# Two token mixers in a fused float32 block: when the row scans run, in which order the mLSTM's heads go, and where the output projection's first terms stand

## The chip, the cores and the metric
The kernel runs on one core of one Trainium2 chip. The time is the device time of one execution in microseconds; the runs of the kernel before are 2084.67 (median), 2084.38 and 2088.93.

## The reference
All arithmetic is float32, on 256 tokens of width 1024. Two layers each do a feed-forward (SwiGLU, inner width 2816), a token mixer and a second feed-forward, each with modulation, residual and layer norm; then an attention block and a gated linear attention block follow. The change touches the two token mixers alone:

```python
qkv_a, a_a, b_a, z_a, qkv_b, qk_c, v_c, i_c, f_c, o_c = jnp.split(h @ w_in, IN_SPLITS, axis=-1)
qa, ka, va = jnp.split(causal_conv_silu(qkv_a, gdn_conv), 3, axis=-1)   # 6 heads of 64
qa, ka = l2norm(split_heads(qa)), l2norm(split_heads(ka))
oa = gated_delta_rule(qa, ka, va, g, beta)        # then rms over a head, norm gain, times silu(z_a)
ob = moba_attention(qb, kb, vb)                   # here: causal softmax attention, 4 heads
hc = mlstm_chunkwise(qc, kc, vc, i_pre, logf)     # 6 heads; num / max(|den|, exp(-m))
hc = hc * sigmoid(o_c)                            # then mean and variance over a head, gain
return jnp.concatenate([oa, ob, hc], axis=-1) @ w_out
```

## The kernel before, in words
Each engine has its own instruction stream, written out by hand, with semaphores between them; `step(...)` looks up the count at which a named step of another engine is done. All weights come as one stream of 1 MB chunks (2048 floats on each of 128 partitions) through a ring of 8 slots. The sync engine issues the loads in order, chunk n as soon as chunk n - 8 has been released. Every float32 product is issued as `mm`, two matmul instructions in the trace, all at L335; transposes are at L338. ScalarE's operations are all at L1253, VectorE's at L1720 (tensor with tensor), L1723 (with a scalar), L1726 (both) and L1729 (copy).

A mixer (`mixer(l)`, one function per engine, m = 1 and m = 4) works feature-major: a chunk of `w_in` gives two tiles of 128 features by 256 tokens.
- **Start.** The chunks of WIN_FIRST (12: gate rows; 0 to 4: the delta rule's q, k, v) are projected one after the other. VectorE convolves each tile (four operations, `conv`), ScalarE applies silu. `rows` (L2009) is VectorE's work on the gate rows: scans, maxima, a reciprocal. The l2 norm of q and k is square (ScalarE, "l2sq"), sums over a head (TensorE, "l2", six products), plus epsilon (VectorE, "l2e"), then reciprocal root as Ln and Exp (ScalarE, "ri", each with its own activation table). TensorE issues l2 behind the fourth chunk after 12 (i == 4), then the last chunk, then waits for "rows", the convolutions and "l2e" before it transposes the rows and spreads them over partitions ("pairs", "gb").
- **Middle.** The delta rule's 64 by 64 triangular inverses are built by five doubling steps (li = 1 to 5) of 48 small products and two half-updates each; the steps after it ("x" 6, "y" 6, "vn0", "s", "ks", "vn1", "oa", "oa_sum") are a chain between TensorE and VectorE or ScalarE.
- **Work beside the chain.** `BESIDE` is a list of pieces of independent work; each engine's `fill(n)` does the next n of them, and the places of the calls fix the order. Piece s writes its result to bank 0 (s even) or bank 7 (s odd) and waits until piece s - 2 has been read ("fread"). Kinds: p = half a chunk projected (p15 only 128 columns); ms, mt, mo = attention's scores, transposes, output; lm = exp of the mLSTM's minus maximum for a pair of heads; lb = one head's decay, two tiles of 256 and 128 columns; ls = its scores; ln and ld = numerator and denominator of a pair of heads. At the pieces numbered in `MOD_AT`, a column of the next sublayer's modulation is taken from a chunk on which GpSimd or VectorE worked, and that chunk's slot becomes free.
- **Tail.** For ld of pair p, VectorE takes max(-den, exp(-m)), max(den, that), a reciprocal (L1992), numerator times that, times the output gate ("lh"): five operations. After the third pair come "lmu" (head means), "lvar" (head variances) and the output projection: of its 8 terms in k, five (delta rule and attention) are issued first for all four chunks of `w_out`, the last three when "mixed" is there. Banks 0 to 3 hold its result.

Of the kernel before, what the change touches and what calls it, by code (L numbers as in the profile page):

```python
# [13 lines left out]
P = 128  # L14
# [24 lines left out]
WIN_FIRST = [12, 0, 1, 2, 3, 4]  # L39
WIN_LATER = [6, 7, 13, 8, 9, 10, 14, 15, 5, 11]  # L40
BESIDE = (["p6.0", "p6.1", "p7.0", "p7.1", "p13.0", "p13.1"]
# [4 lines left out]
HALVES = 4  # L46
FFN_ORDER = [c for p in range(FT // 2 + 1) for c in
             ((("w13", 2 * p), ("w13", 2 * p + 1)) if p < FT // 2 else ()) + ((("w2", p - 1),) if p else ())]
AFTER_MS = {"p8.0": 0, "p8.1": 1, "p9.0": 2, "p9.1": 3}
MOD_AT = {1: 2, 5: 3, 11: 4, 15: 5, 19: 6, 23: 7}  # L50
ROW_A, ROW_B, ROW_I, ROW_F = 0, 32, 64, 96
# [39 lines left out]
def build(nc, stream, cols_in, tab_in, wg_in, xt_in, ct_in, out, marks):  # L91
# [3 lines left out]
    with ExitStack() as ctx:  # L95
# [46 lines left out]
        def step(*key):  # L142

            return marks[key][1] if marks else 1
# [184 lines left out]
        def _(eng):  # L329
# [138 lines left out]
            def mixer(l):  # L468
# [25 lines left out]
                def part(name):  # L494
# [10 lines left out]
                    if kind == "p":  # L505
# [4 lines left out]
                        if t:  # L510
                            held[0] = held_w[1]
                            release()
                            found["beside", m, s] = found["chunk", held[0]]
                            return
                    elif kind == "ms":
                        h = int(what)
# [17 lines left out]
                    elif kind == "lm":  # L534
                        p = int(what)
                        mm(beside(s, 256), table("pair", P * p, P)[ROW_I:ROW_I + 32, :], r_nm[ROW_I:ROW_I + 32, :], True, True)
                    elif kind == "lb":
                        h = int(what)
                        mm(beside(s, 256), each(ident[ROW_I:ROW_I + 32, ROW_I + h:ROW_I + h + 1], 128)[:, 0, :], r_max[ROW_I:ROW_I + 32, :], True, True)
                    elif kind == "ls":  # L540
                        h = int(what)
                        o = beside(s)
                        eng.wait_ge(scalar_done, step("silu", m, 21))
                        mm(o[:, 0:256], head(qkv[:, 12:15], h, 0), head(qkv[:, 9:12], h), True, True)
                        mm(o[:, 256:384], head(qkv[:, 12:15], h, 1), head(qkv[:, 9:12], h, 1), True, True)
                    else:
                        for h in (2 * int(what), 2 * int(what) + 1):
                            o = half(beside(s, 256), h)
                            eng.wait_ge(vector_done, step("lp", m, h))
                            for st in range(2):  # L550
                                lhs = vt[:, st, 256 + 64 * h:256 + 64 * h + 64] if kind == "ln" else ones[:, 0:64]
                                if st == 0:
                                    mm(o, lhs, l_w[:, h, 0:256], True, False, free=True)
                                else:
                                    mm(o[:, P:T], lhs, l_w[:, h, 256:384], False, True, free=True)
                    last[0].then_inc(tensor_done, 1)
# [9 lines left out]
                for i, ch in enumerate(WIN_FIRST):  # L566
# [9 lines left out]
                    if i == 4:  # L576
# [6 lines left out]
                        done.named("l2", m)  # L583
                        mod_cols(m + 1, 1)

                eng.wait_ge(vector_done, step("rows", m))
# [131 lines left out]
                done.named("vn1", m)  # L718
                fill(2)
                eng.wait_ge(vector_done, step("vn1s", m))  # L720
# [8 lines left out]
                done.named("oa", m)  # L729
                fill(4)  # L730
                eng.wait_ge(scalar_done, step("oa_sq", m))
# [3 lines left out]
                done.named("oa_sum", m)  # L735
                fill(len(BESIDE) - at["n"])
                eng.wait_ge(vector_done, step("lh", m, 2))
# [3 lines left out]
                done.named("lmu", m)  # L741

                w_out, w_held = [], []
                eng.wait_ge(vector_done, step("oa_done", m))
                eng.wait_ge(scalar_done, step("mo", m, 1))
                for ch in range(4):
                    w_out.append(tiles(take("wout", l, ch), 256))
                    w_held.append(held[0])
                    for t in range(2):
                        for k in range(5):  # L750
                            mm(bank(ch, 256 * t, 256 * t + 256), w_out[ch][:, k, P * t:P * t + P], xa[:, k, CS], k == 0 and t == 0, False, free=True)
                    if ch == 0:
                        eng.wait_ge(scalar_done, step("lsq", m))
                        for t in range(3):
                            mm(banks(4, 1024)[:, 256 * t:256 * t + 256], blk, tiles(l_sq, 256)[:, t], True, True)
                        last[0].then_inc(tensor_done, 1)
                        done.named("lvar", m)
                eng.wait_ge(vector_done, step("mixed", m))
# [489 lines left out]
        def _(eng):  # L1248
# [107 lines left out]
            def mixer(l):  # L1356
# [18 lines left out]
                def part(s):  # L1375
# [5 lines left out]
                    if kind == "p":  # L1381
# [5 lines left out]
                        if ch < 13:  # L1387
                            gate_or_copy(2 * ch + t, beside(s, 256), *key)
                        else:
                            n = 256 if ch < 15 else 128  # L1390
                            act(vt[:, t, 256 * (ch - 13):256 * (ch - 13) + n], beside(s, n), ACT.Copy, *key).then_inc(scalar_done, 1)
                    elif kind == "ms":
                        h = int(what)
# [45 lines left out]
                act(g_sq, W(QKV, 1536), ACT.Square, "l2sq", m).then_inc(scalar_done, 1)  # L1439
                silu(6)  # L1440
                silu(7)
                eng.wait_ge(vector_done, step("l2e", m))
                rsqrt(g_tt, "ri", m)
                eng.wait_ge(tensor_done, step("proj", m, 5))
                gate_or_copy(9, bank(6, 256, 512), "proj_read_a", m, 5)
                silu(8)
                eng.wait_ge(tensor_done, step("pairs", m))
                eng.wait_ge(vector_done, step("kb", m))
# [23 lines left out]
                for b in range(2):  # L1472
                    act(tiles(g_tt, 128)[64 * b:64 * b + 64, :, 64 * b:64 * b + 64], tiles(g_tp, 64)[64 * b:64 * b + 64], ACT.Copy, "t", m, 7, b).then_inc(scalar_done, 1)
                fill(4)
                fill(8)
                eng.wait_ge(tensor_done, step("oa", m))
# [234 lines left out]
        def _(eng):  # L1711
# [211 lines left out]
            def mixer(l):  # L1923
# [28 lines left out]
                def part(s):  # L1952
# [23 lines left out]
                    elif kind == "ls":  # L1976
# [4 lines left out]
                        found["lp", m, h] = found[key]  # L1981
                    elif kind == "ld":
                        p = int(what)
                        sn = BESIDE.index(f"ln{p}")
# [3 lines left out]
                        stt(l_em[:, u], beside(s, 256), -1.0, l_em[:, u], MUL, ALU.max).then_inc(vector_done, 1)  # L1988
                        eng.wait_ge(vector_done, done.count)
                        tt(l_em[:, u], beside(s, 256), l_em[:, u], ALU.max, *key).then_inc(vector_done, 1)  # L1990
# [3 lines left out]
                        tt(l_h[:, u], beside(sn, 256), l_em[:, u], MUL, "fread", m, sn).then_inc(vector_done, 1)  # L1994
                        eng.wait_ge(vector_done, done.count)
# [43 lines left out]
                for i, ch in enumerate(WIN_FIRST):  # L2039
# [26 lines left out]
                tt(g_vb, qkv[:, 6:9], tiles(banks(4, 768), 256), MUL, "kb", m).then_inc(vector_done, 1)  # L2066
                fill(1)
                eng.wait_ge(tensor_done, step("gb", m))
# [59 lines left out]
                copy(g_vn[:, 1, :], bank(1, 0, 384), "vn1s", m).then_inc(vector_done, 1)  # L2128
                fill(6)
                eng.wait_ge(tensor_done, step("oa_sum", m))  # L2130
                ts(o_rstd, banks(2, 768), 1.0 / HD, MUL, EPS, ADD, "oa_e", m).then_inc(vector_done, 1)
                fill(2)
                eng.wait_ge(scalar_done, step("oa_r", m))
# [452 lines left out]
```

## Time and profile before
| what | value |
|---|---|
| median of the runs | 2084.67 us |
| profiled execution | 2086.86 us |
| its span | 2085.1 us, 30584 instructions |
| TensorE busy (matmul) | 1923.1 us, 92% |
| VectorE, ScalarE, GpSimd busy | 1268.2, 695.6, 131.5 us |
| mean granted clock | 0.948 |
| first mixer, TensorE | about 270.5 to 543.3 us of the span |
| second mixer, TensorE | about 986 to 1256 us |

The span is from the first to the last instruction. A granted clock of 1.00 is TensorE's 2.4 GHz and 0.50 its 1.2 GHz. "Busy" is the time in which an engine has an instruction under way. In a timeline each line is a merged run of like instructions: start, length, engine, what it writes and reads, shape, count, and in brackets the idle time before it and what ended that.

### The profile page before, as it was taken

How to read it: one execution, taken by the hardware profiler on the slowest of the kernel's cores; microseconds unless marked ns; L12 is line 12 of the kernel's file. 1: busy time of each engine (PE TensorE's matmuls, PEld its weight loads, DVE VectorE, ACT ScalarE, POOL GpSimd, SP SyncE). 2: the span in 40 equal slices, each digit the busy share in tenths (PEclk: the TensorE clock that was granted, in tenths of full speed). 3: DMA queues.
4: the chain of work that ended last, by engine and by line, in shares of the span. 5: the costliest groups of instructions: out<-in, count | busy, mean ns of one | idle time of the engine just before them, and what ended most of it. 6: DMA issues, size and time to landing. Idle time of an engine off the chain costs nothing.

```text
span 2085.1 us, 30584 instructions
## 1 busy us (share of the span) xinstructions
PE 1923.1 (92%) x12976; PEld 1629.2 (78%) x12976; DVE 1268.2 (61%) x2247; ACT 695.6 (33%) x918; POOL 131.5 (6%) x68
## 2 busy tenths in 40 slices
PE   5999978997899989998899988999899999899998
PEld 5999967885799979997778767999765555435896
DVE  2877654523497777776546137999697567224812
ACT  1433233322533344333323226333332243123422
POOL 0000063300000000000532000000000000000000
PEclk9999988995999999999999779999899999999999
DMA  8667612430267746664224204766344020212200
GB/s 322 260 256 283 249 61 102 183 142 0 101 269 277 259 166 243 243 242 182 108 115 165 100 7 166 282 250 247 140 182 182 0 81 1 83 61 91 71 21 21
DMA packets 47112, 323.81 MB, mean 155 GB/s; under 512 B 4944, under 2 KB 8144, under 8 KB 8192
## 3 DMA queue, kind: packets, MB, share of 16 engines
q1 hardware_dynamic: 46976, 321.85, 40.7%
q8 instruction: 103, 1.69, 0.3%
q14 instruction: 33, 0.27, 0.0%
HBM read 320.78 MB, written 1.05 MB: 154 GB/s over the span
## 4 chain that ended last, share of the span: by engine, by line
PE 84%; DVE 11%; ACT 3%; issue 1%; DMA 1%; SPq 0%; DVEq 0%; ACTq 0%
PE ps L335 83%; DVE wk L1726 4%; DVE wk L1720 2%; DVE wk L1723 2%; ACT wk L1253 2%; PE ps L338 1%; DVE low L1720 1%; DMA ring<-in_stream_dram 1%; ACT L1253 1%; DVE wk L1992 1%; ACT xa L1253 0%; DVE tab L1720 0%; DVE wk L1729 0%; ACT res L1253 0%; ACT xhi L1253 0%
## 5 line engine op out<-in xcount | busy, mean ns | idle before, releaser
L335 PE MATMUL ps<-xa,ring 128*128 128x256 f32 (+1 forms) x1776 | 487.5, 434 | 19.3 <-ACT res L1253 13.2
L335 PEld LDWEIGHTS ps<-xa,ring 128*128 128x128 f32 x1776 | 343.4, 195 | 151.5 <-issue 93.8
L335 PE MATMUL ps<-xhi,low 128*128 128x256 f32 x1408 | 387.8, 283 | 0.0
L335 PE MATMUL ps<-xhi,whi_wk 128*128 128x256 f32 x1088 | 306.7, 293 | 20.0 <-ACT xhi L1253 20.0
L1253 ACT ACTIVATE wk<-ps 128x256 f32<-128x256 f32 (+5 forms) x223 | 110.1, 501 | 626.6 <-PE ps L335 540.4
L335 PE MATMUL ps<-xlo,whi_wk 128*128 128x256 f32 x1088 | 297.6, 282 | 0.0
L335 PEld LDWEIGHTS ps<-xhi,low 128*128 128x128 f32 x1408 | 262.5, 190 | 0.0
L1253 ACT ACTIVATE whi_wk<-ring 128x2048 fp32r<-128x2048 f32 x100 | 191.0, 1913 | 199.0 <-PE ps L335 102.8
L335 PE MATMUL ps<-wk 64*64 64x64 f32 (+8 forms) x2712 | 237.6, 276 | 11.9 <-DVE wk L1720 6.4
L1726 DVE SCALAR_TENSOR_TENSOR wk<-ring,sc,wk 128x256 f32<-128x256 f32 x600 | 243.8, 477 | 0.0
L335 PEld LDWEIGHTS ps<-wk 64*64 64x64 f32 (+4 forms) x2712 | 178.3, 154 | 73.2 <-issue 35.8
L1720 DVE TENSOR_TENSOR low<-ring,whi_wk 128x2048 fp32r<-128x2048 f32 x100 | 228.4, 2284 | 0.0
L335 PEld LDWEIGHTS ps<-xhi,whi_wk 128*128 128x128 f32 x1088 | 209.7, 197 | 21.7 <-issue 21.7
L1253 ACT ACTIVATE wk<-wk 128x256 f32<-128x256 f32 (+8 forms) x157 | 103.8, 683 | 307.4 <-DVE wk L1726 198.7
L335 PEld LDWEIGHTS ps<-xlo,whi_wk 128*128 128x128 f32 x1088 | 201.1, 189 | 0.0
L335 PE MATMUL ps<-hhi,low 128*128 128x256 f32 x704 | 198.3, 282 | 0.0
L335 PE MATMUL ps<-wk,tab 128*128 128x256 f32 (+5 forms) x442 | 145.1, 492 | 57.1 <-DVE wk L1720 32.8
L335 PEld LDWEIGHTS ps<-wk,tab 128*128 128x128 f32 (+3 forms) x442 | 92.7, 228 | 95.6 <-DVE wk L1720 36.5
L1720 DVE TENSOR_TENSOR wk<-wk,ps 128x256 f32<-128x256 f32 (+3 forms) x134 | 61.7, 476 | 161.0 <-ACT wk L1253 126.4
L335 PE MATMUL ps<-hlo,whi_wk 128*128 128x256 f32 x512 | 144.7, 283 | 0.0
L335 PE MATMUL ps<-hhi,whi_wk 128*128 128x256 f32 x512 | 144.3, 282 | 0.0
L1720 DVE TENSOR_TENSOR wk<-wk 128x512 f32<-128x512 f32 (+7 forms) x161 | 120.5, 765 | 26.7 <-ACT wk L1253 16.8
(108 smaller groups left out, 2484.8 us busy)
## 6 DMA issues: line engine op xcount, KB each, us to landing
ring<-in_stream_dram SPq DMA_DIRECT2D x302, 1024.0 KB, 5.2
tab<-in_tab_dram SPq DMA_DIRECT2D x1, 1632.0 KB, 7.1
res<-in_xt_dram SPq DMA_DIRECT2D x1, 1024.0 KB, 9.5
res<-in_ct_dram SPq DMA_DIRECT2D x1, 1024.0 KB, 7.4
out_dram<-wk SPq DMA_DIRECT2D x2, 512.0 KB, 3.0
cols<-in_cols_dram SPq DMA_DIRECT2D x1, 242.5 KB, 2.6
tab<-in_wg_dram SPq DMA_DIRECT2D x1, 96.0 KB, 2.2
```

The lines of the kernel that those rows point to most:

```text
L335: last[0] = nc.tensor.matmul(o, l, r, start=start, stop=stop, skip_group_check=free)
L338: last[0] = nc.tensor.transpose(o, i, ident[0:k, 0:k])
L1253: return nc.scalar.activation(o, i, f, **kw)
L1720: return do(v.tensor_tensor(o, a, b, op), *key)
L1723: return do(v.tensor_scalar(o, a, s1, None, op0) if op1 is None else v.tensor_scalar(o, a, s1, s2, op0, op1), *key)
L1726: return do(v.scalar_tensor_tensor(out=o, in0=a, scalar=s, in1=b, op0=op0, op1=op1), *key)
L1992: do(v.reciprocal(l_em[:, u], l_em[:, u])).then_inc(vector_done, 1)
```

## The change
The constants at the top of the file change, and the places of `fill` on all three engines:
- `BESIDE`: p15.0 and p15.1 become one piece, q15, which projects both halves into one bank and stands behind ls4; p5 and p11 move two places forward. lm0 to lm2 come first, then the heads in the order of the diff. ln and ld become lx: numerator (columns 0 to 255) and denominator (256 to 511) in bank 0, the two heads of a pair issued in turns. The list has 47 pieces where it had 51.
- `WIN_LATER` and `MOD_AT` follow: chunk 15 is streamed last, and the modulation columns stand two pieces later.
- TensorE takes two pieces (p6.0, p6.1) ahead of the wait for "rows". The calls behind the delta rule's steps become 2, 2, 2, 1 and 2, and 7 behind "oa_sum".
- VectorE does `rows` and then "l2e" behind the convolutions of chunk 2, and chunk 3's afterwards. ScalarE does silu of tiles 6 and 7 after "ri" and the gate of the last chunk.
- The output projection's five first terms: chunk 1 stands ahead of lx2, chunk 2 behind it, half of chunk 3 behind "lmu", the rest behind "lvar".

```diff
-WIN_LATER = [6, 7, 13, 8, 9, 10, 14, 15, 5, 11]
+WIN_LATER = [6, 7, 13, 8, 9, 10, 14, 5, 11, 15]
...
-             "mt3", "p15.0", "mo1", "p15.1", "p5.0", "p5.1", "p11.0", "p11.1"]
-          + ["lm0", "lb0", "lb1", "ls0", "lb2", "ls1", "lm1", "lb3", "ls2", "ln0", "ld0", "lb4", "ls3", "lb5", "lm2", "ls4", "ln1", "ld1",
-             "ls5", "ln2", "ld2"])
+             "mt3", "p5.0", "mo1", "p5.1", "p11.0", "p11.1"]
+          + ["lm0", "lm1", "lm2", "lb0", "lb1", "ls0", "ls1", "lb2", "lx0", "lb3", "ls2", "lb4", "lb5", "ls3", "ls4", "q15", "lx1", "ls5", "lx2"])
...
-MOD_AT = {1: 2, 5: 3, 11: 4, 15: 5, 19: 6, 23: 7}
+MOD_AT = {3: 2, 7: 3, 13: 4, 17: 5, 21: 6, 25: 7}
...
+                    elif kind == "q":
+                        ch, o = int(what), beside(s, 256)
+                        w = weights(6 + WIN_LATER.index(ch), ch)
+                        for t in range(2):
+                            project(o[:, P * t:P * t + P], w, ch, t)
+                        release()
...
-                        for h in (2 * int(what), 2 * int(what) + 1):
-                            o = half(beside(s, 256), h)
+                        pair = (2 * int(what), 2 * int(what) + 1)
+                        for h in pair:
                             eng.wait_ge(vector_done, step("lp", m, h))
+                        for n in range(2):
                             for st in range(2):
...
+                                for h in pair:
+                                    o = half(bank(0, 256 * n, 256 * n + 256), h)
+                                    lhs = ones[:, 0:64] if n else vt[:, st, 256 + 64 * h:256 + 64 * h + 64]
...
+                fill(2)
 
                 eng.wait_ge(vector_done, step("rows", m))
...
                 done.named("vn1", m)
-                fill(2)
+                fill(1)
...
                 done.named("oa", m)
-                fill(4)
+                fill(2)
...
-                fill(len(BESIDE) - at["n"])
+                fill(len(BESIDE) - 1 - at["n"])
...
+                eng.wait_ge(vector_done, step("oa_done", m))
+                eng.wait_ge(scalar_done, step("mo", m, 1))
+                early(1, 0)
+                early(1, 1)
+                fill(1)
+                early(2, 0)
+                early(2, 1)
                 eng.wait_ge(vector_done, step("lh", m, 2))
...
                 done.named("lmu", m)
...
+                early(3, 0)
+                eng.wait_ge(scalar_done, step("lsq", m))
...
+                early(3, 1)
+                early(0, 0)
+                early(0, 1)
                 eng.wait_ge(vector_done, step("mixed", m))
...
                 act(g_sq, W(QKV, 1536), ACT.Square, "l2sq", m).then_inc(scalar_done, 1)
-                silu(6)
-                silu(7)
                 eng.wait_ge(vector_done, step("l2e", m))
                 rsqrt(g_tt, "ri", m)
                 eng.wait_ge(tensor_done, step("proj", m, 5))
                 gate_or_copy(9, bank(6, 256, 512), "proj_read_a", m, 5)
+                silu(6)
+                silu(7)
                 silu(8)
+                fill(2)
...
-                    if ch == 1:
+                    if ch == 2:
                         rows()
-                    if ch == 3:
                         eng.wait_ge(tensor_done, step("l2", m))
```

Here `early(ch, t)` takes chunk ch of `w_out` when t is 0 and issues the five products of its half t.

## Rows read from the trace of the kernel before

**Rows 1.** The page: the span, and the granted clock in 40 slices, in tenths.
```profile
span 2085.1 us, 30584 instructions
...
PEclk9999988995999999999999779999899999999999
```

**Rows 2.** Windows of the first mixer: busy per engine (count), clock, DMA share, GB/s.
```profile
330.80:349.50 18.70, 18.64 (x63) 13.63 (x63) 7.72 (x9) 5.29 (x15) 4.11 (x3) 0.73 0.12 40
...
362.50:441.10 78.60, 77.43 (x1082) 66.99 (x1081) 38.63 (x82) 24.20 (x49) 16.16 (x8) 1.00 0.46 176
...
456.50:478.00 21.50, 21.44 (x90) 14.79 (x90) 4.44 (x11) 4.85 (x10) 0.00 (x0) 0.59 0.14 50
478.00:513.60 35.60, 25.04 (x86) 16.34 (x85) 17.00 (x28) 7.78 (x13) 0.00 (x0) 0.55 0.00 0
513.60:543.30 29.70, 29.70 (x135) 25.70 (x133) 3.19 (x5) 6.90 (x6) 0.00 (x0) 0.98 0.22 83
```

**Rows 3.** Timeline of TensorE at the first mixer's start: start, us, what, idle before.
```profile
314.62 5.46 PE L335 MATMUL ps<-wk,tab 128*128 128x256 f32 x12 [6.24 <-ACT wk L1253]
...
320.45 7.15 PE L335 MATMUL ps<-xa,ring 128*128 128x256 f32 x32
330.79 0.66 PE L338 MATMUL ps<-tab,wk 128*128 128x128 f32 x2 [3.19 <-DVE wk L1726]
331.38 5.90 PE L335 MATMUL ps<-wk,tab 32*128 32x256 f32 x12
337.21 5.47 PE L335 MATMUL ps<-xa,ring 128*128 128x256 f32 x16
```

**Rows 4.** The same of the second mixer's start.
```profile
1030.16 4.57 PE L335 MATMUL ps<-wk,tab 128*128 128x256 f32 x12 [7.31 <-ACT wk L1253]
...
1044.92 0.41 PE L338 MATMUL ps<-tab,wk 128*128 128x128 f32 x2 [2.83 <-DVE wk L1726]
1045.26 4.11 PE L335 MATMUL ps<-wk,tab 32*128 32x256 f32 x12
1049.30 6.11 PE L335 MATMUL ps<-xa,ring 128*128 128x256 f32 x16
```

**Rows 5.** Timeline of TensorE in the first mixer's tail.
```profile
437.63 2.02 PE L335 MATMUL ps<-ring,xa 128*128 128x128 f32 x16 [0.65 <-DVE mod L1720]
...
456.98 1.13 PE L335 MATMUL ps<-wk,tab 32*128 32x256 f32 x4
...
488.97 1.22 PE L335 MATMUL ps<-wk,tab 32*128 32x256 f32 x2 [3.28 <-DVE wk L1720]
...
497.34 1.55 PE L335 MATMUL ps<-wk,tab 128*64 128x256 f32 x8
502.11 3.40 PE L335 MATMUL ps<-wk 64*128 64x256 f32 x10 [3.22 <-DVE wk L1720]
...
510.90 2.93 PE L335 MATMUL ps<-wk,tab 128*128 128x256 f32 x6 [3.68 <-DVE wk L1720]
```

**Rows 6.** Windows of the tail at half clock, and the one ahead of them.
```profile
460.20:484.20 24.00, 24.00 (x80) 15.94 (x79) 4.32 (x11) 4.88 (x9) 0.00 (x0) 0.50 0.02 8
487.60:514.90 27.30, 18.65 (x60) 12.59 (x61) 14.17 (x23) 3.28 (x8) 0.00 (x0) 0.50 0.00 1
...
456.80:460.20 3.40, 3.34 (x28) 2.54 (x22) 1.29 (x4) 2.63 (x5) 0.00 (x0) 1.00 0.72 260
```

**Rows 7.** Timeline of VectorE there: first and last of `rows` (13 instructions), and l2e.
```profile
298.38 0.93 DVE L1726 SCALAR_TENSOR_TENSOR wk<-wk 128x256 f32<-128x256 f32 x1
...
306.56 1.74 DVE L2037 RECIPROCAL wk<-wk 32x256 f32<-32x256 f32 x1
...
320.12 1.76 DVE L1723 TENSOR_SCALAR wk<-ps 128x1536 f32<-128x1536 f32 x1 [3.39 <-PE ps L335]
```

**Rows 8.** Timeline of ScalarE: the reciprocal root's first operation and its last table load.
```profile
321.90 1.48 ACT L1253 ACTIVATE wk<-wk 128x1536 f32<-128x1536 f32 x1 [3.37 <-DVE wk L1723]
...
326.20 1.28 ACT L1253 ACT_TABLE_LOAD   x1
```

More of the change, by code:

```diff
@@ L514, in part @@
                             return
+                    elif kind == "q":
[4 more added lines that the diff above has]
+                        release()
+                        found["beside", m, s] = found["chunk", held[0]]
+                        return
                     elif kind == "ms":
@@ L546, in part @@
                     else:
-                        for h in (2 * int(what), 2 * int(what) + 1):
-                            o = half(beside(s, 256), h)
+                        pair = (2 * int(what), 2 * int(what) + 1)
+                        for h in pair:
                             eng.wait_ge(vector_done, step("lp", m, h))
+                        for n in range(2):
                             for st in range(2):
[L551 to L555, printed above, removed]
+                                for h in pair:
+                                    o = half(bank(0, 256 * n, 256 * n + 256), h)
+                                    lhs = ones[:, 0:64] if n else vt[:, st, 256 + 64 * h:256 + 64 * h + 64]
+                                    if st == 0:
+                                        mm(o, lhs, l_w[:, h, 0:256], True, False, free=True)
+                                    else:
+                                        mm(o[:, P:T], lhs, l_w[:, h, 256:384], False, True, free=True)
                     last[0].then_inc(tensor_done, 1)
@@ L735, in mixer, with early @@
                 done.named("oa_sum", m)
-                fill(len(BESIDE) - at["n"])
+                fill(len(BESIDE) - 1 - at["n"])
+                w_out, w_held = {}, {}
+                def early(ch, t):
+                    if t == 0:
+                        w_out[ch] = tiles(take("wout", l, ch), 256)
+                        w_held[ch] = held[0]
+                    for k in range(5):
+                        mm(bank(ch, 256 * t, 256 * t + 256), w_out[ch][:, k, P * t:P * t + P], xa[:, k, CS], k == 0 and t == 0, False, free=True)
+                eng.wait_ge(vector_done, step("oa_done", m))
[5 more added lines that the diff above has]
+                early(2, 1)
                 eng.wait_ge(vector_done, step("lh", m, 2))
@@ L741, in mixer @@
                 done.named("lmu", m)
[L743 to L757, printed above, removed]
+                early(3, 0)
+                eng.wait_ge(scalar_done, step("lsq", m))
+                for t in range(3):
+                    mm(banks(4, 1024)[:, 256 * t:256 * t + 256], blk, tiles(l_sq, 256)[:, t], True, True)
+                last[0].then_inc(tensor_done, 1)
+                done.named("lvar", m)
+                early(3, 1)
+                early(0, 0)
+                early(0, 1)
                 eng.wait_ge(vector_done, step("mixed", m))
@@ L1391, in part @@
                             act(vt[:, t, 256 * (ch - 13):256 * (ch - 13) + n], beside(s, n), ACT.Copy, *key).then_inc(scalar_done, 1)
+                    elif kind == "q":
+                        eng.wait_ge(tensor_done, step("beside", m, s))
+                        act(vt[:, :, 512:640], tiles(beside(s, 256), P), ACT.Copy, *key).then_inc(scalar_done, 1)
                     elif kind == "ms":
@@ L1473, in mixer @@
                     act(tiles(g_tt, 128)[64 * b:64 * b + 64, :, 64 * b:64 * b + 64], tiles(g_tp, 64)[64 * b:64 * b + 64], ACT.Copy, "t", m, 7, b).then_inc(scalar_done, 1)
-                fill(4)
-                fill(8)
+                fill(11)
                 eng.wait_ge(tensor_done, step("oa", m))
@@ L1981, in part @@
                         found["lp", m, h] = found[key]
-                    elif kind == "ld":
+                    elif kind == "lx":
                         p = int(what)
-                        sn = BESIDE.index(f"ln{p}")
+                        num, den = bank(0, 0, 256), bank(0, 256, 512)
                         u = slice(256 * p, 256 * p + 256)
@@ L1987, in part @@
                         eng.wait_ge(scalar_done, step("em", m, p))
-                        stt(l_em[:, u], beside(s, 256), -1.0, l_em[:, u], MUL, ALU.max).then_inc(vector_done, 1)
+                        stt(l_em[:, u], den, -1.0, l_em[:, u], MUL, ALU.max).then_inc(vector_done, 1)
                         eng.wait_ge(vector_done, done.count)
-                        tt(l_em[:, u], beside(s, 256), l_em[:, u], ALU.max, *key).then_inc(vector_done, 1)
+                        tt(l_em[:, u], den, l_em[:, u], ALU.max).then_inc(vector_done, 1)
                         eng.wait_ge(vector_done, done.count)
@@ L1993, in part @@
                         eng.wait_ge(vector_done, done.count)
-                        tt(l_h[:, u], beside(sn, 256), l_em[:, u], MUL, "fread", m, sn).then_inc(vector_done, 1)
+                        tt(l_h[:, u], num, l_em[:, u], MUL, *key).then_inc(vector_done, 1)
                         eng.wait_ge(vector_done, done.count)
@@ L2066, in mixer @@
                 tt(g_vb, qkv[:, 6:9], tiles(banks(4, 768), 256), MUL, "kb", m).then_inc(vector_done, 1)
-                fill(1)
+                fill(3)
                 eng.wait_ge(tensor_done, step("gb", m))
@@ L2128, in mixer @@
                 copy(g_vn[:, 1, :], bank(1, 0, 384), "vn1s", m).then_inc(vector_done, 1)
-                fill(6)
+                fill(3)
                 eng.wait_ge(tensor_done, step("oa_sum", m))
                 ts(o_rstd, banks(2, 768), 1.0 / HD, MUL, EPS, ADD, "oa_e", m).then_inc(vector_done, 1)
-                fill(2)
+                fill(4)
                 eng.wait_ge(scalar_done, step("oa_r", m))
```

## Prediction

> **What bounds the kernel now.** I read the page first: TensorE is busy nearly throughout, so only its waits and its clock can be won. One slice of the granted clock stands at 5 and two at 7; they lie in the two mixers [rows 1]. The windows of the first mixer by stage show where [rows 2]: the middle (362.5 to 441.1, the delta rule's doubling steps between projections) is busy 77.4 of 78.6 us at full clock; from 456.5 to 513.6 the clock stands at 0.59 and 0.55 and TensorE is idle for 10.6 us; from 513.6 on it is dense again. The timeline of TensorE gives the waits by name. At the mixer's start it waits 6.24 us before the l2 sums (314.62), for ScalarE's square, and 3.19 us before the row transposes and pair sums (330.79), for the last convolution; l2, pairs and half a projection then run at the lower level [rows 3]. The second mixer repeats it: 7.31 and 2.83 us [rows 4]. In the tail it waits 3.28, 3.22 and 3.68 us, each time for VectorE's reciprocal and products of one pair of heads [rows 5]. Half-clock stretches hold 24.00 and 18.65 us of TensorE's busy time in the tail [rows 6].
>
> **The start: rows behind the third chunk.** Before the change VectorE does `rows` from 298.38 to 308.3 [rows 7], so the third chunk's convolutions, whose projection was done by about 301.4 (64 matmul instructions from 294.3 in 14 us), start 7 us late, and with them silu, square and l2. Afterwards the convolutions run 301.5 to 305.6 (two tiles, 2.07 us each), square ends at about 307.5, and TensorE ends the fourth projection at 308.4: l2 follows without a wait. The 6.24 us go (7.31 in the second mixer).
> `rows` then takes 305.7 to 315.6 and l2e 1.76 us to 317.4 [rows 7]. ScalarE's reciprocal root with its two table loads takes what it took between 321.90 and 327.48 [rows 8], 5.6 us: to 323.1, gate copy to 323.5. The last convolution, 0.45 us behind that, ends at 326.0. TensorE meanwhile has l2 (2.75 us at full clock), modulation columns 0.4, the fifth projection 7.0 and, moved ahead, p6.0 and p6.1 with 7.0 (32 instructions take 7.15 [rows 3]): it comes at 325.5. About 0.8 us of the second wait stays; 2.4 us go (2.0).
> **The clock of these steps.** l2 falls from 5.46 to 2.75, transposes and pairs from 6.56 to 3.3, p6.0 from 5.47 to 3.6: 7.9 us [rows 3]; in the second mixer 4.57, 4.52 and 6.11 give 5.6 [rows 4]. The pairs use 32 rows of the array, and the short wait stands before them, so I put one short stretch of half clock behind them, at 1.5 us (from nothing to 3.5). The start brings 6.24 + 2.4 + 7.9 - 1.5 = 15.0 and 7.31 + 2.0 + 5.6 - 1.5 = 13.4, in all **28.4 us**.
> The moved silu(6), silu(7) (0.42 us each) and the fourth chunk's convolutions have slack up to 323.5. VectorE's chain behind pairs and kk is as long as before, with a whole p13 (7 us) on TensorE over it in place of p7.
> **DMA and the queues.** A ring slot's next load waits for its release. The second modulation chunk is released behind l2, so ch7 and ch13 are asked for at about 311.5 instead of 320.6 and are there long before use at 330 and 345. The later modulation columns move two places later in the list, and the work moves two places too; chunks 9, 10 and 14 keep some 10 us. The sync queue loses nothing; wout is taken 1, 2, 3, 0, so the next feed-forward's first slots come 2.6 us later, with its first four chunks long landed: nothing. The wait for the modulation vector (0.65 us [rows 5]) stands behind p11.0 now and goes: **1.3 us** in both.
>
> **The tail.** p5 and p11 (14 us of dense work) leave the places behind y6 and vn0 and fill the doubling steps; ch15 (4.06 us) moves the other way, to between the head pairs. The steps vn0, s, ks, vn1, oa of the delta rule then have only fills of some 1 us between them: `lm`, `lb` of 0.43 us (four instructions take 1.13 us [rows 5]) and `ls` of 0.64 us at full clock. Those cover VectorE's 0.4 to 1.0 us copies nearly: I leave 0.5 us of waits.
> The three pair waits, 10.2 us [rows 5], go for these reasons: the reciprocal chain (3.6 us) of pair 0 lies beside oa, that of pair 1 beside ls5 and the output projection's chunk 1 (20 instructions, 4.3 us), that of pair 2 beside chunk 2. lmu's and lvar's chains lie beside five or more products each. What is late next is `mixed`, about level with TensorE.
> The clock decides the rest. Before, it falls at 460.2, when TensorE has been busy 3.34 of 3.40 us [rows 6], with products of 32 and 64 rows; so small work without a gap is enough. After the change such work begins 1.6 us before vn0 and lasts until ch15: about 19 us at full clock, 33 at half. The fall came 3.7 us behind the last dense projection (456.5); I expect it 4 us behind y6, and the full level again when ch15 is half done, 37 us in all, which costs 17 us; before, the 42.65 busy us cost about 20 (half, less weight loads and switches that do not stretch). Per mixer: 10.2 + 3.0 - 0.5 = 12.7, in both **25.4 us**.
> **Heads in turns.** Numerator and denominator of a pair in one bank, heads alternating: the row at 497.34 has eight instructions of both heads in 1.55 us at half clock [rows 5], where one head's four take 2 x 0.43 + 2 x 0.21 = 1.28. The heads run side by side already; I take nothing. Two steps joined save two switches of shape, 0.3 us, inside the rounding. Should they run one behind the other in other rows, the turn would give 0.64 us a step at full clock, 7.7 us in all. The Trainium skill (TensorE: Matmul & The Clock Gate, Part 3) calls matmuls strictly first in, first out; read so that a head waits for the other's four, it would give those 7.7 us. The row disagrees.
>
> **Sum.** 28.4 + 1.3 + 25.4 = 55.1 us. The profiled execution took 2086.9 (span 2085.1): 2031.8. The median of the runs is 2.2 lower: **2029.5**.
>
> **The rivals.**
> *The clock stays high in the tail* (0.10). For it: TensorE has no gaps left there, the heads of a pair fill both halves of the array. Against it: the fall at 460.2 with no gap [rows 6]. It would return the 17 us of each mixer: 2029.5 - 34 = 1996; half of it, 2012. The Trainium skill (the same page, Why this matters for your kernels) ties the fall to gaps between bursts of matmuls; by that rule this case would be the one to come. The trace disagrees, with 3.34 of 3.40 us busy.
> *More half clock or a later chain than I see* (0.24). Pairs and gb hold the clock down for all of p6, p7 and gb (4 us more), the stretch in the tail runs past ch15 into lx1 and ls5 (4 us more), and VectorE's l2e comes late enough to leave 2 us before the pairs: 10 us a mixer, 2050. For it: the stretch from 330.8 to 349.5 has 0.73 now [rows 2], with p6.0 slow behind the pairs [rows 3].
> *Slower: the middle loses the clock* (0.04). Its 77.4 busy us run at 1.00 now because each doubling step of 64 by 64 products stands between full-array projections; the first fill changes from p13 (7 us, dense) to ms0 with p8.0 (4.3 us). If the half level took hold there, each us of it would cost nearly one. It decides from 28 us a mixer on; taken whole, +77 a mixer less 55 gives 2186; for 40 us a mixer, 2110. Against it: pairs of just this kind (ms, mt with half a chunk) stand in the other steps now, at 1.00 [rows 2].
> *It doesn't do what it says* (0.03). If ch7 or ch15's chunk came late, or ScalarE's order held the silu of the last tile, TensorE would wait as long in other places: 2085.
>
> **How the numbers follow.** The main case has 0.59. Range: bounds of the half-clock terms (2 x (1.5 + 17) with some 40% either way) are +-15; below it takes in half of the first rival, above the second rival: 2007 to 2052, leaving out some 0.2. A measurement tells 0.2% (4 us) from no change. Faster 0.93, same 0.03, slower 0.04.
>
> **What would show it.** l2 right behind the fourth projection, 12 instructions in under 3 us; pairs with a wait below 1 us, behind p6.1; t0t about 10 us earlier relative to the mixer's first matmul; a clock near 0.5 from vn0 to ch15; no wait over 0.6 us between the pairs; each mixer about 245 us from first to last matmul instead of 273. The prediction is wrong if the wait moves to the pairs, if the tail shows 1.00, or if the middle shows less than 0.95.

## Result and profile after

| | before | after |
|---|---|---|
| median of the runs (four each) | 2085.47 us | 2005.18 us (2003.26 to 2007.60) |
| ratio | | 0.9607, 95% interval 0.9591 to 0.9623 |
| profiled execution, its span | 2086.86, 2085.1 us | 2003.26, 2001.5 us |
| first mixer, TensorE | 270.5 to 543.3, 272.8 us | 269.7 to 500.9, 231.2 us |
| second mixer, TensorE | 986.0 to 1256.2, 270.2 us | 943.4 to 1174.0, 230.6 us |
| time at half clock within the span (its records begin at 60 us) | 218.5 us | 123.0 us |

The kernel is 80 us faster; 55 were forecast, and the time lies 2 us below the stated range. The two mixers give 41.6 and 39.6 us, 81.2 of the 83.6 by which the two profiled executions differ.

The page of the kernel after, where it answers to [rows 1]:

```profile
span 2001.5 us, 30584 instructions
...
PE 1881.4 (94%) x12976; PEld 1605.1 (80%) x12976; DVE 1253.7 (63%) x2247; ACT 694.2 (35%) x916; POOL 131.3 (7%) x68
...
PEclk9999989989899989998999889999899999999999
```

The windows of its first mixer, cut where its stages end: at t0t (the start of the doubling steps), at the end of y6, at the end of oa, at the first early terms of the output projection, at the mixer's end. Columns as in [rows 2]:

```profile
269.70:350.70 81.00, 80.81 (x386) 69.28 (x386) 44.63 (x70) 30.27 (x54) 49.45 (x24) 0.97 0.27 104
350.70:431.40 80.70, 80.52 (x1082) 69.21 (x1081) 38.08 (x82) 26.70 (x51) 16.15 (x8) 1.00 0.47 185
431.40:456.20 24.80, 24.74 (x123) 18.03 (x121) 9.39 (x18) 3.84 (x10) 0.00 (x0) 0.66 0.10 40
456.20:468.70 12.50, 11.65 (x77) 9.11 (x76) 6.28 (x13) 7.62 (x12) 0.00 (x0) 1.00 0.11 31
468.70:500.90 32.20, 32.17 (x156) 27.34 (x156) 10.45 (x16) 6.90 (x6) 0.00 (x0) 1.00 0.17 65
```

The middle is as dense as before (80.5 of 80.7 us at 1.00). Where [rows 2] had clocks of 0.59 and 0.55 and 10.6 us without work, one window stands at 0.66 and nearly nothing is idle.

TensorE's timeline at the start, to be read against [rows 3]:

```profile
306.98 2.75 PE L334 MATMUL ps<-wk,tab 128*128 128x256 f32 x12
...
309.93 14.06 PE L334 MATMUL ps<-xa,ring 128*128 128x256 f32 x64
323.83 0.38 PE L337 MATMUL ps<-tab,wk 128*128 128x128 f32 x2
324.14 3.17 PE L334 MATMUL ps<-wk,tab 32*128 32x256 f32 x12
327.24 3.72 PE L334 MATMUL ps<-xa,ring 128*128 128x256 f32 x16
```

l2 stands right behind the fourth projection, at full clock (2.75 us for 5.46), then the fifth projection and p6 in one run of 64 instructions, then transposes and pairs without a wait (3.17 us for 5.90 in the K = 32 products). The second mixer has one dip behind its pairs: the half chunk at 1007.19 takes 5.39 us.

The tail, against [rows 5]:

```profile
431.44 1.13 PE L334 MATMUL ps<-wk,tab 32*128 32x256 f32 x4
...
448.44 1.49 PE L334 MATMUL ps<-wk,tab 128*64 128x256 f32 x8
449.72 6.53 PE L334 MATMUL ps<-wk 128*64 128x128 f32 x36
...
460.79 1.45 PE L334 MATMUL ps<-wk 64*128 64x256 f32 x8 [0.52 <-DVE wk L1745]
462.36 3.84 PE L334 MATMUL ps<-ring,xa 128*128 128x128 f32 x32
466.13 0.87 PE L334 MATMUL ps<-wk 128*64 128x256 f32 x8
466.83 0.82 PE L334 MATMUL ps<-wk,tab 128*64 128x256 f32 x8
...
468.73 4.58 PE L334 MATMUL ps<-xa,ring 128*128 128x256 f32 x20 [0.23 <-DVE xa L1751]
473.24 0.87 PE L334 MATMUL ps<-wk 128*64 128x256 f32 x8
```

No wait inside the mixer is over 0.6 us. The pair waits of 3.28, 3.22 and 3.68 us have become 0.52 (ls3) and 0.23 (for "oa_done"). lx takes 0.70 us from numerator to denominator and 0.75 more.

Windows of the half-clock stretches of the tail, and of the work ahead of the first:

```profile
434.60:451.70 17.10, 17.04 (x75) 12.66 (x74) 6.18 (x15) 2.78 (x7) 0.00 (x0) 0.50 0.00 1
...
431.40:434.60 3.20, 3.20 (x21) 2.59 (x20) 1.41 (x2) 1.06 (x3) 0.00 (x0) 1.00 0.74 307
1110.50:1124.10 13.60, 13.54 (x56) 10.54 (x54) 4.11 (x11) 2.34 (x6) 0.00 (x0) 0.50 0.00 0
```

They last 17.1 and 13.6 us (elsewhere rounded to 13.7); I had put 37 in each mixer.

### The profile page after: what moved, and what is told of

Read it like the earlier page. It is cut to its first block, busy times and chain, and to the rows that moved or that the text cites. A ratio compares the mean times of both kernels' runs of the same rounds, so it can differ in the third digit from the quotient of the medians.

```text
span 2001.5 us, 30584 instructions
## 1 busy us (share of the span) xinstructions
PE 1881.4 (94%) x12976; PEld 1605.1 (80%) x12976; DVE 1253.7 (63%) x2247; ACT 694.2 (35%) x916; POOL 131.3 (7%) x68
## 4 chain that ended last, share of the span: by engine, by line
PE 87%; DVE 8%; ACT 3%; issue 1%; DMA 1%; SPq 0%; DVEq 0%; ACTq 0%
PE ps L334 85%; DVE wk L1751 3%; ACT wk L1275 2%; DVE wk L1745 2%; PE ps L337 1%; DVE wk L1748 1%; DVE low L1745 1%; ACT L1275 1%; DMA ring<-in_stream_dram 1%; ACT xa L1275 0%; DVE tab L1745 0%; ACT res L1275 0%; DVE wk L1754 0%; ACT xhi L1275 0%; DVE small L2223 0%
## 5 line engine op out<-in xcount | busy, mean ns | idle before, releaser
L334 PEld LDWEIGHTS ps<-xa,ring 128*128 128x128 f32 x1776 | 339.3, 193 | 149.3 <-issue 92.8
L1275 ACT ACTIVATE wk<-ps 128x256 f32<-128x256 f32 (+4 forms) x221 | 109.7, 504 | 612.0 <-PE ps L334 526.6
L334 PE MATMUL ps<-wk 64*64 64x64 f32 (+10 forms) x2712 | 221.3, 268 | 6.5 <-ACT wk L1275 5.1
L334 PEld LDWEIGHTS ps<-wk 64*64 64x64 f32 (+4 forms) x2712 | 170.4, 151 | 60.7 <-issue 30.3
L1275 ACT ACTIVATE wk<-wk 128x256 f32<-128x256 f32 (+8 forms) x157 | 103.4, 682 | 270.5 <-DVE wk L1751 173.9
L334 PE MATMUL ps<-wk,tab 128*128 128x256 f32 (+4 forms) x442 | 124.7, 440 | 29.2 <-DVE wk L1745 19.0
L334 PEld LDWEIGHTS ps<-hhi,low 128*128 128x128 f32 x704 | 132.6, 188 | 0.0
```

What stands on the lines that cost most here:

```text
L334: last[0] = nc.tensor.matmul(o, l, r, start=start, stop=stop, skip_group_check=free)
L1275: return nc.scalar.activation(o, i, f, **kw)
```

## Experiments

Each run was measured beside the kernel before, whose median was then 2086.8 to 2087.35 us; the ratios are to that.

**The start alone.** Put on the kernel before:

```diff
-MOD_AT = {1: 2, 5: 3, 11: 4, 15: 5, 19: 6, 23: 7}
+MOD_AT = {3: 2, 7: 3, 13: 4, 17: 5, 21: 6, 25: 7}
...
                         mod_cols(m + 1, 1)
+                fill(2)
...
                 done.named("oa", m)
-                fill(4)
+                fill(2)
...
-                    if ch == 1:
+                    if ch == 2:
                         rows()
-                    if ch == 3:
```
with silu 6 and 7 behind "ri" as in the change, and the places of `fill` on ScalarE and VectorE to match; the lists of pieces stay the old ones.

> The kernel before with the start of the change alone: rows behind chunk 2's convolutions, silu 6 and 7 behind the reciprocal root, two pieces ahead of the wait for rows; the tail keeps the old list, with two pieces less behind oa. Theory (the two parts add up): the two waits and the half-clock stretches of the start go, 18 us a mixer, so 2085 - 36 = 2049. Rival (the start's gain is 15 us a mixer as forecast, and the tail carries the rest): 2055. Rival (work only moves, the wait comes back behind y6 or vn0): 2070 or more.

Measured: 2053.44 us (2052.28 to 2053.64), ratio 0.9839 (0.9824 to 0.9853), 34 us less. That is 17 us a mixer. The tail keeps its three waits (3.25, 3.22, 3.68 us) and its long stretch at half clock, 27.3 us in the first mixer (440.4 to 467.7) and 23.9 in the second. TensorE's timeline from vn1 and oa on:

```profile
451.23 13.09 PE L335 MATMUL ps<-wk 128*64 128x128 f32 x48
464.25 4.02 PE L335 MATMUL ps<-wk,tab 128*128 128x256 f32 x14
471.52 1.21 PE L335 MATMUL ps<-wk,tab 32*128 32x256 f32 x2 [3.25 <-DVE wk L1722]
```

In that stretch TensorE has no wait at all (27.24 of 27.30 us busy): steady work alone did not bring the level back for 27.3 us.

**The tail alone.** The kernel after with the old start, and four pieces behind x 6:

```diff
-                    if ch == 2:
+                    if ch == 1:
                         rows()
+                    if ch == 3:
...
                 done.named("x", m, 6)
-                fill(2)
+                fill(4)
```

> The changed kernel with the old start; four pieces behind x 6 instead of two, so that the tail is the new one. Theory (additive): the tail gives 22 us a mixer, so 2085 - 45 = 2040, and its stretch at half clock is 14 to 17 us long, as in the changed kernel. Rival (the short stretch is owed to the start's shift in time): it lasts over 30 us and the time is 2055 or more.

Measured: 2045.16 us (2044.72 to 2049.59), ratio 0.9805 (0.9790 to 0.9820), 42 us less. Both stretches at half clock are 17.1 us. So the shortness of the stretch belongs to the new tail and not to the start. The parts add to 76 of 80 to 82 us.

**Heads one behind the other.** The kernel after with

```diff
                         for n in range(2):
-                            for st in range(2):
-                                for h in pair:
+                            for h in pair:
+                                for st in range(2):
```

> The changed kernel with lx's heads one behind the other (head outside, token half inside) instead of in turns. Theory (the two heads' products lie in different column halves and run side by side in either order): 2005, within 0.1%. Rival (the turn is what makes them overlap and what filled the array ahead of oa): 0.64 us a step and a longer stretch at half clock, 2012 to 2025.

Measured: 2009.37 us, but from 2004.65 to 2012.27, ratio 0.9622 (0.9602 to 0.9641); the interval overlaps that of the change. In its trace the steps themselves are the same:

```profile
449.31 1.55 PE L334 MATMUL ps<-wk,tab 128*64 128x256 f32 x8
...
468.90 0.88 PE L334 MATMUL ps<-wk 128*64 128x256 f32 x8
469.60 0.87 PE L334 MATMUL ps<-wk,tab 128*64 128x256 f32 x8
```

1.55 us for the eight instructions of the denominators at half clock (1.49 with turns), 0.87 at full clock (0.82). That is 0.05 us a step, 0.3 in all. The execution has 143.8 us at half clock where that of the change has 123.0: 3.4 more in the second mixer's stretch (17.1 us), a dip of 3.4 at 463.5 to 466.9 beside ch15, the rest mostly outside the mixers. The turn is not what made the change fast; whether it has a part in this, the runs don't tell.

**Early terms of the output projection back.** early(1, ..) and early(2, ..) behind lmu:

```diff
-                early(1, 0)
-                early(1, 1)
                 fill(1)
-                early(2, 0)
-                early(2, 1)
                 eng.wait_ge(vector_done, step("lh", m, 2))
...
                 done.named("lmu", m)
+                early(1, 0)
+                early(1, 1)
+                early(2, 0)
+                early(2, 1)
                 early(3, 0)
```

> The changed kernel with the first terms of the output projection's chunks 1 and 2 behind lmu instead of between the last pairs. Theory (they cover VectorE's chain of the last two pairs): two waits of some 3.6 us a mixer come back, and the clock falls once more behind them, 3 us: 2005 + 20 = 2025. Rival (the new order of the heads alone had removed the waits): 2008 or less.

Measured: 2031.40 us (2027.41 to 2031.73), ratio 0.9730 (0.9715 to 0.9744), 26 us more than the change. Its TensorE timeline:

```profile
474.48 1.55 PE L334 MATMUL ps<-wk 128*64 128x256 f32 x8 [3.40 <-DVE wk L1751]
475.78 1.53 PE L334 MATMUL ps<-wk,tab 128*64 128x256 f32 x8
480.99 2.93 PE L334 MATMUL ps<-wk,tab 128*128 128x256 f32 x6 [3.68 <-DVE wk L1745]
483.71 12.64 PE L334 MATMUL ps<-xa,ring 128*128 128x256 f32 x50
```

Two waits, 3.40 and 3.68 us, and the products around them at half clock: that level lasts from 473.5 to 487.1, with 9.0 us of work in it. The second mixer waits 4.29 and 3.68 us and has another such stretch of 13.7 us, again with 9.0 us of work. So the early terms are worth 26 us of the 80: 15 are waits, and most of the other 11 is clock (at most 4.5 us for each of these two stretches, and the dip beside ch15 and a stretch 3.4 us longer besides).

**The first pair behind oa.** lx0 moves by one place of `fill`, from ahead of oa to behind it (on ScalarE too):

```diff
                 done.named("vn1", m)
-                fill(1)
+                fill(0)
...
                 done.named("oa", m)
-                fill(2)
+                fill(3)
```

> The changed kernel with lx0 (numerator and denominator of the first pair) behind oa instead of ahead of it. Theory (lx0's two heads fill both column halves of the array at half clock just ahead of oa, and that brought the full level back at 451.7): the half-clock stretch lasts through oa, 25 us instead of 17.1 and 13.7, which costs 3 to 4 us a mixer; the reciprocal chain of pair 0 then stands ahead of ls2, a wait of 2 to 3 us: 2005 + 13 = 2018. Rival (the level comes back after a while of work without a gap, whatever it is): stretches of 17 us as before, only the wait is added, 2010.

Measured: 2026.88 us (2026.58 to 2031.41), ratio 0.9721 (0.9704 to 0.9737), 22 us more. The windows of its stretches in the two mixers, and its timeline from oa on:

```profile
434.40:461.70 27.30, 26.59 (x106) 18.30 (x106) 5.18 (x13) 3.59 (x8) 0.00 (x0) 0.50 0.01 2
1120.50:1147.80 27.30, 26.59 (x106) 17.86 (x104) 5.53 (x15) 3.59 (x8) 0.00 (x0) 0.50 0.00 1
```

```profile
448.68 11.51 PE L334 MATMUL ps<-wk 128*64 128x128 f32 x44 [0.65 <-DVE wk L1754]
459.98 2.25 PE L334 MATMUL ps<-wk,tab 128*64 128x256 f32 x10
464.70 1.27 PE L334 MATMUL ps<-wk 64*128 64x256 f32 x4 [2.47 <-DVE wk L1745]
...
1145.34 2.61 PE L334 MATMUL ps<-wk,tab 128*64 128x256 f32 x10
```

Both stretches are 27.3 us long (the one over oa in the kernel before is 24.0), and oa is at half clock to its end (11.51 us with lx0's numerators behind it, where the change has 6.53 for oa alone). The waits are 0.65 and 2.47 us. The stretch's end moved with lx0: the level came back at 461.7 and 1147.8, 1.7 and 2.5 us after lx0's denominators had started behind oa (459.98, 1145.34), as it did in the change 3.3 and 2.0 us after they had started ahead of it (448.44, 1122.06). The run has one flaw: lx0's move also opens the wait of 0.65 us ahead of oa, inside the stretch. That the wait is not what kept the level down is shown by the kernel before (24.00 of 24.00 us busy) and by start_only (27.24 of 27.30): without lx0 ahead of oa the stretch is long without any wait too. Here a move of 2.6 us of work by one place costs 11 us a mixer, of which 3 are waits.

**More dense work ahead.** Four full-array products, not used by anything, behind y6:

```diff
                 done.named("y", m, 6)
+                for _ in range(4):
+                    mm(bank(3, 0, 256), blk, xa[:, 0, XS], True, True)
                 fill(2)
```

> The changed kernel with four more full-array products (128 by 128 by 256, result unused, in a bank that is free then) behind y6 in each mixer: 1.7 us each at full clock. Theory (it is the narrow products that let the clock fall): the fall comes one stretch later, 3.4 us, which gives back about 1.7 us and pays for the added work: 2005, between 2002 and 2008. Rival (the fall is set by something else, the products are only added): 2008.5 with stretches as long as before.

Measured: 2011.00 us (2006.20 to 2015.89), ratio 0.9638 (0.9613 to 0.9663). Two of its executions took 2006 and two 2015 to 2016 us. In the profiled one (2006.55) the stretches are 13.7 us in both mixers, from 437.9 and 1113.7; in the change they begin at 434.6 and 1110.5. The fall came 3.3 us later, as the theory wants, but the return did not come sooner with lx0's products, which are themselves 1.1 us later: 451.6 in the first mixer (451.7 in the change) and 1127.4 instead of 1124.1 in the second, where nothing was gained. No gain is shown, and the forecast of 2002 to 2008 failed; the interval overlaps that of the change, so a loss is not shown either.

**oa in rounds.** The 18 products of oa in another order, in the kernel after (two measurements) and in the kernel before:

```diff
+                def oa_out(h, c):
...
+                for p in range(3):
+                    for c in range(2):
+                        for h in (2 * p, 2 * p + 1):
+                            u = 2 * h + c
+                            mm(oa_out(h, c), g_vn[:, c, 64 * h:64 * h + 64], g_att[:, P * u:P * u + P], p % 2 == 0 and c == 0, c == 0, free=True)
                 for h in range(6):
-                    for c in range(2):
...
-                        mm(o, g_vn[:, c, 64 * h:64 * h + 64], g_att[:, P * u:P * u + P], True, c == 0)
-                        if c:
-                            mm(o, head(S, h), head(g_qd, h), False, True)
+                    mm(oa_out(h, 1), head(S, h), head(g_qd, h), False, True, free=True)
```

> The changed kernel with oa's 18 products in another order: first the 12 of 128 rows and 64 columns with the two heads of a pair in turns, then the 6 of 64 rows. Theory (column halves run side by side when neighbours in the queue lie in different halves and no change of shape stands between): oa falls from 6.5 and 6.0 us to some 2.5, with ls2 still behind lx0's chain: 3.5 us a mixer less, 1998. Rival (the gain comes back as a wait for VectorE's chain of pair 0 or for the square of oa): 2003 to 2005.

> The kernel of the run oa_rounds again, in five rounds, beside the next one on the same chip: 2000, 1998 to 2002, and 0.2 to 0.3% faster than the changed kernel's 2005.

> The kernel before with oa's 18 products in the order of the run oa_rounds, nothing else. Theory (the order alone makes the column halves run side by side): oa takes about 10.0 us at half clock in each mixer there and falls to some 4.5, so 2086 - 11 = 2075; the tail's stretch at half clock stays over 20 us. Rival (it pays only with lx0 ahead of it): over 2082.

Measured: 2000.39 us (1998.91 to 2004.90), ratio 0.9591 (0.9576 to 0.9605), and again 2000.54 us (1999.11 to 2004.95), 0.9588 (0.9567 to 0.9609). The change has 2005.18 and 0.9607 (0.9591 to 0.9623): two medians 5 us lower, with intervals that overlap that of the change. The timeline of the first of them:

```profile
446.10 1.30 PE L334 MATMUL ps<-wk,tab 128*64 128x256 f32 x8
447.23 2.28 PE L334 MATMUL ps<-wk 128*64 128x128 f32 x36
...
450.63 0.92 PE L334 MATMUL ps<-wk 64*128 64x256 f32 x4 [0.50 <-DVE wk L1748]
```

oa falls from 6.53 to 2.28 us, but part of that is the clock: in this execution the first mixer's stretch was only 6.8 us long (17.1 in the second) and ended ahead of oa. In oa_rounds5, where the stretches are 17.1 and 13.7 us as in the change, oa takes 3.43 and 2.55 us against 6.53 and 6.04: 3.1 and 3.5 us less. A wait for lx0's chain (0.50 us here) returns a part. The run changes two things at once, the turns of the heads and the changes of shape (eleven inside oa became one); what each is worth, it does not tell. On the kernel before: 2068.49 us (2066.45 to 2076.73), 0.9916 (0.9886 to 0.9947), 18 us less where 11 were expected. There oa was wholly at half clock, and the quicker products let the clock return at 470.8 instead of 484.2; both stretches over oa are 10.2 us, where they were 24.0 and 23.9. No lx0 stands ahead of oa there: the level came back within oa itself, 3.3 us after its first product (467.5), now that its products keep both column halves at work. The order is worth more where the clock is low.

**A half chunk between the small steps.** oa_rounds with p11.1 between vn0 and s:

```diff
-             "mt3", "p5.0", "mo1", "p5.1", "p11.0", "p11.1"]
-          + ["lm0", "lm1", "lm2", "lb0", "lb1",
+             "mt3", "p5.0", "mo1", "p5.1", "p11.0"]
+          + ["lm0", "lm1", "lm2", "lb0", "p11.1", "lb1",
...
                 done.named("x", m, 6)
-                fill(2)
+                fill(1)
...
                 done.named("y", m, 6)
-                fill(2)
+                fill(3)
```

> oa_rounds with p11.1 (half a chunk, 3.6 us of full-array products) taken from behind x 6 and put between vn0 and s. Theory (narrow products in a row let the clock fall, dense ones ahead of and between them delay the fall or end it): the stretch at half clock shrinks from 6.8 to 17.1 us to below 10 us in both mixers, 3 to 4 us less each where it was 17: 1995. Rival (the fall comes at the same place and p11.1 itself then runs at half): no gain or a loss of up to 3 us a mixer, 2000 to 2006.

Measured: 1999.40 us (1996.94 to 2006.16), ratio 0.9588 (0.9566 to 0.9609). The time at half clock in each tail is 10.2 us (6.8 and 3.4) where oa_rounds5 has 17.1 and 13.7, but the moved half chunk is what runs in it:

```profile
432.90 6.56 PE L334 MATMUL ps<-xa,ring 128*128 128x256 f32 x16
```

6.56 us instead of 3.6. Less half clock with dense work in it came to the same time. Both theories had a part; no gain is shown.

## Why the prediction was wrong

The direction stood, and the waits went as forecast. The step that failed is the term of the sum for the clock in the tail, "half clock ... 37 us in all, which costs 17 us".

- **The first wait** (6.24 and 7.31 us) went, as forecast. l2 started at 306.98, 37.3 us after the mixer's first product; before it was 44.2.
- **The second wait:** forecast 0.8 us left, measured none in either mixer. I had carried the 9.9 us of `rows` over from [rows 7]; they took 6.5, see below. The last convolution was done at 321.3, 2.5 us ahead of the pairs.
- **The start's clock:** of 7.9 and 5.6 us, 7.5 and 5.2 came (l2, transposes with pairs, and the half chunk behind them). The dip of 1.5 us behind the pairs was absent in the first mixer and there in the second. The start gives 92.0 - 81.0 us and two more pieces done (7.1), 18.1 us; in the second mixer 89.2 - 82.0 + 7.1 = 14.3. Forecast were 15.0 and 13.4.
- **DMA, modulation columns, the queues:** no wait on a chunk inside a mixer, and the 0.65 us wait for the modulation vector is gone.
- **Heads in turns:** nothing, as forecast; 0.3 us by the run with the heads one behind the other.
- **The pair waits:** 10.2 us forecast to go, with 0.5 left; 0.75 are left. Taking their cover away brought back 7.1 and 8.0 us.
- **The clock in the tail:** the fall came where it was put, 3.2 us behind y6, with TensorE busy 3.20 of 3.20 us. What was mis-sized is the return. I let oa hold the level down, because it had done so before, and waited for ch15. But the change puts lx0 straight ahead of oa. Its two heads fill both column halves, and the clock came back at 451.7, 2.0 us after oa's first product had started behind them (449.72). The 74 us of both mixers were 30.7, and the 34 us that they were to cost were at most 15.4: some 19 of the 25 us that the forecast fell short. The run with lx0 behind oa shows it: 27.3 us in both mixers, ended 1.7 and 2.5 us into lx0's denominators. By the rest of my sum with the measured 15.4, the forecast would have been about 2011. The term's price, somewhat under half of the busy time, fits the rows: twelve instructions of 128 x 64 took 1.55 us at full clock (432.55 in the change) and 2.82 at half (445.21 in lx0_late). That weight loads and changes of shape do not stretch, which I gave as the reason, no run shows.

The rival "the clock stays high in the tail" was half true: it named the heads that fill both halves as its reason, and its half-way figure, 2012, is the nearest of all. Its other ground, that no gaps are left, is not borne out: the clock fell without a gap. The mistake of method was to price a whole region with one level, and not to ask which piece of the new order was dense enough to end it. Two slips of arithmetic change nothing: 2031.8 less 2.2 is 2029.6, and the 2186 of "the middle loses the clock" counts from the profiled execution; from the median it is 2184.

The whole account, by the two profiled executions (83.6 us apart, 28.5 more than forecast): 2.4 us outside the mixers, 3.1 and 0.9 in the start, 22.1 in the middle and the tail. These windows hold y6's end to the mixer's end, first before, then after:

```profile
441.10:543.30 102.20, 91.58 (x386) 70.26 (x384) 26.13 (x46) 21.96 (x32) 0.00 (x0) 0.75 0.15 55
431.40:500.90 69.50, 68.56 (x354) 54.49 (x352) 26.12 (x46) 18.36 (x28) 0.00 (x0) 0.88 0.13 50
```

With the middle added and the two moved pieces (7.1 us) taken off, TensorE's busy time fell by 12.8 us in the first mixer and 14.6 in the second, where my sum had 3.0 each for the clock: 21.4 more. The early return of the level explains at most 18.6 of it; the rest, some 3 us, is not divided further.

## What to carry to other kernels

In stretches of narrow products TensorE's clock is part of the schedule. Try a step that fills both column halves ahead of the long narrow one (here its place was worth 22 us, some 6 of them waits), and put products of one shape together, with neighbours in different column halves (oa at like clock: 6.5 us became 3.4; which of the two counts more is open). Cover a chain of small VectorE operations with products that need nothing from it; here that was worth 15 us of waits and some 11 more, mostly clock. When an operation is moved in time, its duration may not move with it: look at what ran beside it.

## What was not expected of the hardware

**Some of VectorE's short operations end only when GpSimd's end.** `rows` took 9.9 us before, 10.2 in tail_only (the old start), and 6.5 us in the change. The same operations in the kernel after, where GpSimd had ended its last operation at 302.8 and is idle until 314.9:

```profile
305.01 0.35 DVE L1748 TENSOR_SCALAR wk<-wk,small 128x256 f32<-128x256 f32 x1
305.40 0.42 DVE L2044 TENSOR_TENSOR_SCAN wk<-tab,wk 128x128 f32<-128x128 f32 x1
...
306.11 0.49 DVE L2048 TENSOR_TENSOR_SCAN wk<-tab,small,wk 128x128 f32<-128x128 f32 x1
```

and in the run tail_only, with GpSimd's operation beside them:

```profile
299.39 2.26 DVE L1746 TENSOR_SCALAR wk<-wk,small 128x256 f32<-128x256 f32 x1
301.68 1.44 DVE L2042 TENSOR_TENSOR_SCAN wk<-tab,wk 128x128 f32<-128x128 f32 x1
...
303.41 0.52 DVE L2046 TENSOR_TENSOR_SCAN wk<-tab,small,wk 128x128 f32<-128x128 f32 x1
```

0.35 against 2.26 us for one operation on 128 x 256, 0.42 against 1.44 for the first scan, and the second scan, past 303.4, is alike again (0.49 and 0.52). GpSimd's three additions lie at 299.1 to 303.7 there. The second mixer of the kernel before has the same, and shows it for the operation ahead as well:

```profile
1010.96 3.60 POOL L2411 TENSOR_TENSOR ring<-ring,sc 128x2048 f32<-128x2048 f32 x1
1014.64 4.56 POOL L2415 TENSOR_TENSOR ring<-ring 128x1024 f32<-128x1024 f32 x3
1012.85 1.99 DVE L1726 SCALAR_TENSOR_TENSOR wk<-wk 128x256 f32<-128x256 f32 x1
1014.94 2.26 DVE L1723 TENSOR_SCALAR wk<-wk,small 128x256 f32<-128x256 f32 x1
```

The first of the three additions ends at 1017.05. So VectorE's two operations end at 1014.84 and 1017.20, 0.28 and 0.15 us behind GpSimd's at 1014.56 and 1017.05. The first of them took 0.93 us in the first mixer, where GpSimd's product ended 0.65 us after it had started, 1.99 here, where that is 1.71 us, and 0.43 in the change with GpSimd idle: its length follows GpSimd's end. Not every operation does this: those that read PSUM take 0.48 us each beside GpSimd's additions (300.27 to 302.84 in the change) and without them. The Trainium skill (GPSIMD Engine Reference, 1. Specifications) says that GpSimd shares its SBUF interfaces with VectorE, with contention for VectorE's instructions in a two-port mode or with two SBUF inputs; the rows agree in kind. No run here took GpSimd's work away alone; the evidence is these ends in three mixers.

**The clock falls and returns without a gap deciding it.** It fell with TensorE busy throughout (3.20 of 3.20 us, 3.34 of 3.40 before) and returned in the midst of steady work. Two profiled executions of one kernel differ in where it falls: in oa_rounds the stretches of the two mixers are 6.8 and 17.1 us, in oa_rounds5 17.1 and 13.7. Executions of one kernel differ by up to 0.4%, and the mean granted clock goes with it (lx_serial: 0.969 at 2004.65 us, 0.965 at 2012.27).
